# Expert row lists by one-hot products, gathered rows transposed by VectorE, three shared down products beside the expert units

## The reference

```python
x = h.reshape(-1, D)                      # 544 tokens
s = sigmoid(x @ w_router); sb = s + router_bias
# of 8 groups of 8 experts the best 4 (sum of their top 2), then the top 8 experts
wsel = wsel / sum(wsel) * 2.5
for e in 64 experts:                      # FF = 256
    y = (silu(x @ w_gate[e]) * (x @ w_up[e])) @ w_down[e]
    routed += gates[:, e:e+1] * y
shared = (silu(x @ ws_gate) * (x @ ws_up)) @ ws_down
return routed + shared
```

## Time and profile before

| | us |
|---|---|
| median of three runs | 1521.06 |
| the profiled execution's own time | 1513.65 |
| its span, first to last instruction | 1511.8 |
| first expert weights sent (L2048) | 812.3 |
| first gate/up product of the units (L2134) | 857.0 |
| last down product of the units (L2142) ends | 1436.7 |

### The profile page before, as it was taken

The page is one execution under the profiler, slowest core; times in us unless marked ns, Lnnn a source line. Parts: engine busy times, 40 slices in busy tenths (PEclk is TensorE's granted clock), DMA queues, the critical chain, the costliest instruction groups (busy, mean ns, idle before and its releaser), DMA issues. The chain is left out here.

```text
span 1511.8 us, 21981 instructions
## 1 busy us (share of the span) xinstructions
PE 1383.9 (92%) x8512; PEld 790.9 (52%) x8512; DVE 562.8 (37%) x1292; ACT 291.6 (19%) x674; POOL 316.0 (21%) x334
## 2 busy tenths in 40 slices
PE   5999999999969999899998799998999999999966
PEld 3776777764657776776454334443344333434322
DVE  1101455453633654445886243211111111111138
ACT  1002233453223222111111011111011111101021
POOL 6000000000069994000054111111112111111100
PEclk9999999999989999989999899999999999999988
DMA  9510410123464443685006789999999999999585
GB/s 338 173 56 8 143 58 1 56 85 112 135 185 138 140 138 94 216 289 185 29 29 180 265 362 396 408 415 417 420 401 401 412 419 389 416 412 420 204 315 226
DMA packets 106804, 358.50 MB, mean 237 GB/s; under 512 B 28837, under 2 KB 31013, under 8 KB 80581
## 3 DMA queue, kind: packets, MB, share of 16 engines
q1 hardware_dynamic: 81288, 301.98, 52.0%
q0 software_dynamic: 15968, 40.61, 7.3%
q10 hardware_dynamic: 9446, 14.51, 2.8%
HBM read 331.49 MB, written 38.15 MB: 245 GB/s over the span
## 5 line engine op out<-in xcount | busy, mean ns | idle before, releaser
L2134 PE MATMUL bank<-arena 128*32 128x512 f32 (+2 forms) x1536 | 335.1, 618 | 19.6 <-DMA arena<-in_w_up 17.7
L2134 PEld LDWEIGHTS bank<-arena 128*32 128x32 f32 (+2 forms) x1536 | 121.1, 138 | 201.3 <-issue 198.5
L2142 PE MATMUL bank<-arena 128*32 128x512 f32 (+2 forms) x768 | 168.6, 598 | 0.7 <-DVE arena L2915 0.7
L2121 POOL DMA_INDIRECT expert_rows<-arena x46 | 46.4, 1008 | 485.4 <-PE bank L2127 418.6
L2909 DVE TENSOR_TENSOR arena<-arena,bank 128x256 f32<-128x256 f32 x46 | 19.4, 421 | 320.7 <-ACT arena L2556 320.7
L1210 PE MATMUL bank<-arena 128*128 128x272 f32 x512 | 128.7, 404 | 1.9 <-ACT arena L1247 1.6
L438 PE MATMUL bank<-arena 128*128 128x272 f32 x480 | 113.8, 400 | 2.8 <-PEq L132 1.9
L2142 PEld LDWEIGHTS bank<-arena 128*32 128x32 f32 (+2 forms) x768 | 55.0, 134 | 110.3 <-issue 109.4
L1210 PEld LDWEIGHTS bank<-arena 128*128 128x128 f32 x512 | 95.8, 193 | 28.0 <-issue 7.1
L438 PEld LDWEIGHTS bank<-arena 128*128 128x128 f32 x480 | 92.9, 194 | 23.1 <-issue 2.8
L668 PE MATMUL bank<-arena 128*128 128x272 f32 x384 | 100.3, 405 | 0.0
(11 more groups left out here) (485 smaller groups left out, 1788.9 us busy)
## 6 DMA issues: line engine op xcount, KB each, us to landing
arena<-in_w_gate SPq DMA_DIRECT2D x64, 1024.0 KB
arena<-in_w_up SPq DMA_DIRECT2D x64, 1024.0 KB
arena<-in_w_down SPq DMA_DIRECT2D x64, 1024.0 KB, 15.3
arena<-in_w_ada SPq DMA_DIRECT2D x12, 2048.0 KB, 9.4
arena<-in_w_in SPq DMA_DIRECT2D x11, 2048.0 KB, 9.9
arena<-expert_rows SPq DMA_DIRECT2D x8, 2048.0 KB, 25.5
gate_logits<-arena ACTq DMA_DIRECT2D x16, 272.0 KB, 3.8
arena<-gate_logits SPq DMA_DIRECT2D x8, 544.0 KB, 5.0
```

The lines of the kernel that those rows point to most:

```text
L2121: return nc.gpsimd.indirect_dma_start(out=y_d, out_offset=bass.IndirectOffsetOnAxis(ap=rows, axis=0), in_=of, in_offset=None, bounds_check ...
L2134: mm = nc.tensor.matmul(out[rows].rearrange("p (a n) -> p a n", a=2), x[:, k, rows], gate_up_slot(n)[:, :, k, :], start=k == 0, stop=k == ...
L2142: mm = nc.tensor.matmul(out[rows, :], h[:, k, rows], down_slot(n)[:, k, 512 * half:512 * half + 512], start=k == 0, stop=k == 1)
```

## The change

1. *Row lists.* Beside each address, a one-hot over experts times the entry's value (`ent_e`, 64 columns) and a one-hot over the place (`ent_p`, 192 columns) is made, by POOL for tiles 0 to 2 and by DVE for tiles 3 and 4. PE's products of the two add up to all lists in PSUM bank 7 (`enter`). DVE copies them (`lists_out`), and `unit_rows` multiplies them by the rank's one-hot `hot`. The scatters to `expert_lists` stay, for the late units only: tile 0's before the one-hots, the other 26 behind the first three gathers. SP holds the first w_down, whose slot `ent_p` uses, until the last list product.
2. *Shared down products.* Tiles 0 and 1 are done ahead of the units, tiles 2 to 4 beside units 0 to 3 (`BESIDE`), and `down(0)` moves behind `up(4)`.
3. *Gathered rows.* PE's `xT`, ACT's and DVE's copies are gone. DVE writes `XT` from `Xg` by 16 transposes of 32 partitions and eight 32x32 blocks each; DVE now waits for the gather.

```diff
+ROWS = 192
@@ load_expert
+            if name == "w_down" and dn is dl[0] and n == 0:
+                sp.wait_ge(list_mm.sem, 2 * PT + 1)
@@ PE
+            def enter(t, half):
+                n = 4 if t < PT else 2
+                pe.wait_ge(ent_made.sem, 2 * t + half + 1) if t < 3 else pe.wait_ge(ent_late.sem, 2 * t + half - 5)
+                for k in range(n):
+                    mm = nc.tensor.matmul(bank[7][E * (k % 2):E * (k % 2) + E, 0:ROWS], ent_e[:, 4 * half + k, :], ent_p[half][:, k, :],
+                                          start=t == 0 and half == 0 and k < 2, stop=t == PT and k >= n - 2)
+                list_mm.inc(mm)
...
             for u in range(NU):
                 if u:
                     hiddenT(u - 1)
-                if u + 1 < NU:
-                    xT(u + 1)
+                if 1 <= u <= len(BESIDE):
+                    shared_step("high", BESIDE[u - 1])
                 gate_up_of(u)
...
+                if u < len(BESIDE):
+                    shared_step("hiddenT", BESIDE[u])
                 if u:
                     down_of(u - 1)
...
+                if u < len(BESIDE):
+                    shared_step("low", BESIDE[u])
@@ POOL
+            def one_hots(t):
+                pool.wait_ge(addr_done.sem, t + 1)
+                if t:
+                    pool.wait_ge(list_mm.sem, 2 * t)
...
+                for k in range(TOPK):
+                    step(TS(ent_e[:, k, :], key[:, t, :], a8[:, t, k:k + 1], short_val[:, t, k:k + 1], ALU.is_equal, ALU.mult))
+                for k in range(TOPK):
+                    ins = TS(ent_p[k // 4][:, k % 4, :], place1, place_of[:, k:k + 1], None, ALU.is_equal)
+                    ent_made.inc(ins) if k % 4 == 3 else step(ins)
...
-            lists_in.inc(nc.gpsimd.indirect_dma_start(out=ranked, out_offset=None, in_=list_d,
-                                                      in_offset=bass.IndirectOffsetOnAxis(ap=order_i.bitcast(U32), axis=0)), 16)
...
             for u in range(RX - 1):
                 gather(u)
+            for t in range(1, NT):
+                enter_tile(t)
@@ DVE
+            def xT(u):
+                dve.wait_ge(g_ld[u % RX].sem, 16 * (u // RX + 1))
...
+                for a in range(4):
+                    slots = slice(QUAD * a, QUAD * a + QUAD)
+                    by_quarter = Xg[u % RX][slots].rearrange("p (k q j) -> p q k j", k=KD, q=4)
+                    for q in range(4):
+                        ins = nc.vector.transpose(XT[u % 2][QUAD * q:QUAD * q + QUAD, :, slots], by_quarter[:, q])
+                ins.then_inc(xt_v.sem, 1)
```

242 lines of the change are left out of this document (127 added, 115 removed).

## The result

The changed kernel takes **1560.63 us** (median of four, 1560.13 to 1562.02), the kernel before 1522.13 in the runs beside it (1520.38 to 1526.91): ratio **1.0235 [1.0197, 1.0274]**. Forecast were 1519.5 us and a range to 1532.

The account below looks back on a forecast made before the run. The units were taken to be bound by DMA, PE just behind. Start +3.8, first units +6.1, stream -8.5 and end -3 summed to -1.6 us, taking 1521.06 to 1519.5 us; range 1502 to 1532.

Parts of the forecast that it names:

- the start of unit 0: Everything ahead of unit 0: up(4) 8.0 us later, the step after it 4.2 us sooner, so unit 0 3.8 us later.
- The bound: In the units: DMA is the bound, with PE less than one unit's slack behind.
- The list products: Ahead of up(4): POOL's one-hots at 10.5 us per tile, bounds 8.5 and 12.4, make up(4) end 8.0 us later, at 843.2.
- POOL is late: Rival on POOL's one-hots: each tile above 10.5 us costs 2 us per 1 us; at 14.5, +8, 1528; chance 0.09.
- From `up(4)` to unit 0: Gather wait and DVE's 16 transposes (7.2 us) between up(4) and unit 0: 17.6 against 21.8 us, 4.2 us sooner.
- The first units: From unit 0's gate/up product to unit 3's: 48.6 instead of 42.5 us, +6.1, with no stall from POOL's 26 scatters.
- The stream: From unit 3's end on: the remaining 208 MB move at 416 instead of 409 GB/s, in 500.0 us, -8.5.
- The first rival: On the stream: the rate is the traffic's own, nothing is gained on 409 GB/s; +6.9, 1528; chance 0.17.
- The end: From the last weights to PE's end: 20 us before, at best 13 to 16 after, taken as -3.
- unit 0 after 868: Sign at the start of unit 0: a start before 855 or after 868 would show the forecast wrong.
- `place(4)` at about 810: Sign on PE ahead of up(4): place(4) at about 810, behind POOL's one-hots, would show the forecast right.

Follow-up runs that it names:

- e3: Changed kernel with the gathers' transposes back on TensorE and their copies on ACT and DVE, row of 26 scatters left in; 1548.59 us, ratio 1.0240.
- e9: Changed kernel with part 2 undone, list products later in PE's queue and the 26 scatters spread one per unit from unit 8; 1530.42 us, ratio 1.0061.
- e1: Changed kernel without the 26 scatters of tiles 1 to 4 between POOL's third and fourth gathers; 1539.63 us, ratio 1.0188.
- e4: Kernel before with only the third part added, its gathered rows transposed on DVE; 1511.77 us, ratio 1.0004.
- e7: Kernel before, with TensorE's transposes, plus a row of 26 repeated scatters behind the third gather; 1543.51 us, ratio 1.0147.
- e8: Kernel before with DVE's transposes, plus a row of 26 repeated scatters behind the third gather; 1542.81 us, ratio 1.0100.
- e12: Kernel before with DVE's transposes, PE and DVE work reordered for a sooner start, down(2) in free banks, most early weights held back; 1522.26 us, ratio 0.9990.
- e13: The version of e12 without holding back weights: only the order of work and the two banks changed; 1526.15 us, ratio 1.0016.
- after_again: Changed kernel run once more, nothing altered; 1559.25 us, ratio 1.0204.
- e2: Changed kernel with the row of scatters split: tiles 1 and 2 ahead of the first gather, the rest one per unit from unit 8; 1543.4 us, ratio 1.0216.
- e5: Changed kernel with part 2 undone: down(2) ahead of the units, tiles 3 and 4 beside them by the old steps; 1550.96 us, ratio 1.0166.
- e10: Changed kernel with the row of 26 scatters replaced by 35 POOL operations of 192 columns; 1537.98 us, ratio 1.0096.
- e11: Changed kernel with the row of 26 scatters moved mid-stream, behind the gather of unit 23; 1566.41 us, ratio 1.0279.
- e15: Changed kernel with a row of only eight scatters behind the third gather, the other 18 one per unit; one run, 1541.82 us.
- e16: The program of e3 run again, unaltered; one run, 1562.01 us.
- e6: Changed kernel with list products later in PE's queue, behind place(4) and the counts, and two shared_hidden steps ahead of DVE's one-hots; 1552.97 us, ratio 1.0168.
- e17: Changed kernel with e9's edits, sort ahead of up(2), tile 2's one-hots on DVE and further reordering around unit 0; 1516.92 us, ratio 1.0030.

## Why the prediction was wrong, point by point

Forecast was a span 1.6 us shorter, and it is 48.5 longer. Of the 50.1 us between them the start of unit 0 has 13.8, the first units 26.7, the stream 7.2 and the end 2.4.

**The bound: right.** The units are bound by DMA. Every kernel without a stall in mid-stream takes 456 to 461 us for the 160 MB from the 40th on, with transposes on either engine.

**The list products: mis-sized, and one step left out.** A tile of one-hots was put at 10.5 us. It measures 13.7 alone and 17.7 for tile 0, above my upper bound of 12.4:

```profile
803.13 0.20 POOL L2635 TENSOR_SCALAR arena<-arena 128x8 f32<-128x8 f32 x1 [3.66 <-PE bank L2328]
...
804.70 5.45 POOL L2641 TENSOR_SCALAR arena<-arena 128x64 f32<-128x64 f32 x8
810.25 6.62 POOL L2643 TENSOR_SCALAR arena<-arena 128x192 f32<-128x192 f32 x8
```

Eight operations of 64 columns take 5.45 us, 0.68 each with the gap, and I had put 0.52 as the most; 192 columns cost little more than 64 and no more than my upper bound, so the fixed part was the error, not the slope. The sum also had PE at tile 1's products as if nothing else stood there. POOL started tile 1 at 803.1 instead of 798.3. That was not tile 0's 17.7 us, which were over at 799.5: PE came to tile 0's products only at 800.1, instead of 796.3 (2.5 of these 3.8 us were there before the change began), and took 2.83 us for them instead of 2.00. Then tile 1 took 3.2 us more than forecast, and `up(1, 4, 6)`, 3.3 us, stands between its products and `place(4)`. So `place(4)` came at 821.7, forecast 809.8, and the order of the experts with it: first weights 829.8 instead of 812.3. I had made that chain end at `up(4)`, without saying what it does to SP. `up(4)` ended at 857.8 instead of 843.2: 14.6 us of error, more than the whole of the start's, since the next step was 0.8 quicker than forecast. My rival "POOL is late" had this mechanism, at 14.5 us a tile, at a price of +8.

**From `up(4)` to unit 0: right.** 16.8 us measured, 17.6 forecast; sixteen transposes took 7.18 us, forecast 7.2. The direct view is DVE's timeline:

```profile
867.34 7.18 DVE L2951 STREAM_TRANSPOSE arena<-arena 32x256 f32<-32x256 f32 x16 [2.06 <-DMA arena<-h_rows,arena]
```

By the Trainium skill, VectorE: DVE Perf Modes, my estimate had been 5.2 us; the trace decides for the row of the plain copy. Its statement, in the section on two Vector instructions with no wait, that an instruction whose output starts in another quadrant is held agrees with the trace: one takes 0.435 us, and they start 0.45 us apart.

**The first units: this step failed.** Forecast +6.1, measured +32.8. "POOL's 26 scatters ... put the fourth gather 33 us behind the third ... I take no stall": I had looked only at the gather that the row delays, and not at the row itself, which made unit 0's product 21.8 us longer. I had no rival for it. In the changed kernel nothing waits long for the fourth gather, since the stall covers it; without the stall it would not have been free, as e3 shows (5.2 us). The other 11.0 us are part 2's, where +6.1 was meant: e9, with it undone, has 41.2 us from unit 0 to unit 3 instead of e1's 54.3. The third shared product's own work on PE was in the sum; its waits for DVE, where the folds now stand behind 7.2 us of transposes, were hardly in it (1.4 us each). PE waits 3.71 us at 939.07 ahead of tile 4's transposes, and the 20th to 40th MB of weights take 9 us longer than in before (10 in e1).

**The stream: this step failed too.** Forecast -8.5, measured between unit 3 and the last weights -1.3. The first rival was right: the rate is the traffic's own. The mean of windows in which PE idled was taken for the rate that DMA has when it is asked for more; it was a choice of good windows. All DMA queues while the weights' queue went from its 40th to its 200th MB, in the kernel before and then in the changed one:

```profile
DMA packets 32394, 188.01 MB, mean 410 GB/s; under 512 B 6095, under 2 KB 6095, under 8 KB 12835
```

```profile
DMA packets 32381, 187.97 MB, mean 410 GB/s; under 512 B 6089, under 2 KB 6089, under 8 KB 12821
```

PE got its waits for weights (43.2 us, forecast 50), and with them a lower granted clock: 0.95 in the windows above, 0.98 in the earlier trace rows. e4, the new transposes alone, says the same: 456.5 us for the 160 MB, before 458.7, ratio 1.0004.

**The end: failed.** Forecast was -3, measured between the last weights and the end -0.6. The last weights of before landed at 1420.7, not at 1415 to 1417. From there to the end of the last down product are 16.0 us before and 15.9 now (1469.8 to 1485.7), so there was no slack to take.

**Against the whole:** 17.6 + 32.8 - 1.3 - 0.6 = 48.5, the difference of the spans. Forecast was 3.8 + 6.1 - 8.5 - 3. With the rate right and all else as I had it the answer would have been 1528, inside the range; the row of scatters (22) and the start (14) put it outside. The signs "unit 0 after 868" and "`place(4)` at about 810" did what they were for. That 38.5 us of medians became 48.5 between the profiles is the luck of which executions were profiled.

**Not in the forecast: before's own start varies.** Before has scatters too, in rows of 8, 16 and 10 beside the routing. From the first scatter to the first weights it takes 49.1 us, and e4 takes 47.2. But e7 and e8, which have the same instructions up to there, take 58.0 and 60.1, and e12 and e13, which hardly change anything ahead of it, 60.6 and 60.1. In e4 ScalarE starts on the logits of tile 3 as soon as PE's last matmul for them has ended; in e8 it waits 10.0 us longer, with DVE and PE waiting behind it, while the row of 16 lasts from 784.5 to 804.6. First e4, then e8:

```profile
782.38 3.31 PE L455 MATMUL bank<-arena 128*128 128x64 f32 x16
785.72 0.23 ACT L2490 ACTIVATE arena<-bank 128x64 f32<-128x64 f32 x1 [6.67 <-PE bank L455]
```

```profile
788.94 2.65 PE L455 MATMUL bank<-arena 128*128 128x64 f32 x16
801.60 0.23 ACT L2492 ACTIVATE arena<-bank 128x64 f32<-128x64 f32 x1 [14.64 <-remote]
```

PE's signal itself comes late: its semaphore event stands at 801.58 in the trace. So the trace from which I forecast was one of two prompt starts among six, and part of the +17.6 is before's luck. The changed kernel has only the first eight scatters there. Its 64.1 us are longer than either kind, but steady: 63.4 to 64.3 in the ten traces with its order of work up to there (changed, after_again, e1 to e3, e5, e10, e11, e15, e16). That before's rows cause the spread is likely; no run takes them out of before alone.

What stays open: why a row of scatters holds TensorE up. While it stands it waits for nothing that the profile shows. In several of the stalls the records of instruction fetches took 1.8 to 3.2 us instead of about 1.0 (in the changed kernel one at 880.59 took 3.2), but in e6's and e16's they took 1.0 and 1.1, and during e11's stall no fetch is recorded. So fetching is not shown to be the cause.

## What to carry to other kernels

In a kernel bound by its weight stream, add up only what moves the first product, what breaks the stream, and what follows its last packet; take the rate from bytes over the whole stream, not from the best windows. Don't put a long row of indirect DMAs on GpSimd beside a product of many small matmuls: spread them one per unit, as e9 and e17 do, in which no gate/up product lasts over 10.0 us. When you compare two profiles, first compare a point ahead of the change: here they were 2.5 us apart before it began. When a new operation stands ahead of a chain in an engine's queue, price every instruction between it and the chain, and follow the chain to the DMA queue that it starts.
